# Eight-head attentions: two PSUM banks in turn for the value products, two instead of three for the turned tiles

## The chip, the cores and the metric

The kernel runs on one core of a Trainium2 chip. The metric is device time in microseconds (us). The engines of the core are TensorE (PE, with its weight loads as PEld), VectorE (DVE), ScalarE (ACT), GpSimd (POOL) and SyncE, which issues transfers. Matrix products leave TensorE into PSUM, which has eight banks of 128 partitions by 512 fp32 numbers; ScalarE and VectorE read them from there.

## The reference, cut to what matters

Two blocks of two layers each work on 1024 tokens of width 1024. Each of the four layers holds an attention with eight query heads of 64 columns, and the change touches these four alone.

```python
# first block, both layers: 8 query heads, 2 heads of keys and values, every key seen
sc = jnp.einsum('bgrqd,bgkd->bgrqk', qblk, kt)
p = jax.nn.softmax(sc, axis=-1)
return jnp.einsum('bgrqk,bgkd->bgrqd', p, vt)
...
# second block, both layers: 8 query heads, 1 head of keys and values, the keys of each row
# chosen (causal, top 256 by an index score)
sc = jnp.where(valid[:, :, None, :], sc, -jnp.inf)
p = jax.nn.softmax(sc, axis=-1).astype(v.dtype)
return jnp.einsum('bthk,btkd->bthd', p, v_sel)
```

The first block also has a differential attention of four heads in each layer. All is computed to fp32 precision, with each fp32 operand of a product split into a high and a low part.

## The kernel before, in words

`heads_phase` computes one attention of eight heads. It is called four times: with the tag `b_` in each layer of the first block, and with the tag `x_` in each layer of the second, where the mask is causal (`causal`). Each engine gets one instruction stream, written out by Python loops that run over the same step number `g` from -5 to 78 (`START` to `END`). The streams meet only in semaphores, so the order inside each stream is fixed.

A step `g` from 0 to 63 is one row tile: 128 queries of one head against all its keys (1024 in `b_`; 128 to 1024, growing with the query tile, in `x_`). Heads go in pairs: steps 16p to 16p+15 are the eight query tiles of the two heads of pair p, in turn. For one row tile:

- TensorE multiplies queries by keys into PSUM banks 0 to 3 (`scores`, line 1143), for two steps at once: the call for steps g+1 and g+2 stands in step g, for odd g.
- VectorE reads the scores, adds mask and minus maximum, and writes a row of probabilities to be (`shift`, line 1002). ScalarE takes the exponent (`exponent`, line 938), VectorE inverts the sum (`invert`, line 1010), GpSimd scales the row (line 1066).

Four row tiles of one head make a column block `n` of 512 queries. Its probabilities are turned (transposed) in tiles of 128 keys by 512 queries: four transposes of 128x128 into one bank (`turn`, line 1104). Each turned tile is then taken out of its bank twice: ScalarE copies the high part (`take`, line 922), and after it VectorE computes the low part from the bank and the high part (`take`, line 985). Two products multiply the tile's high and low part by the values (`product`, lines 1121 and 1122), summed over the block's tiles in one further bank. Once a block is summed, ScalarE reads that bank in two copies (`close`, lines 929 and 932), and GpSimd adds and gates it.

In `b_` every block has eight tiles, two in each step (below: the first and the second of the step). In `x_` the blocks of a head's first 512 queries have four tiles, one in a step, and those of its other 512 have eight, two in a step; so steps 8 to 15 of every 16 have one tile each, and steps 0 to 7 two, from step 8 on. At steps 8, 9, 24, 25, 40 and 41 one further tile is turned ahead of these, a "stack" of queries for the next pair (line 1098, taken out at lines 914 and 977). In `b_` steps 24 and 25 hold a stack of keys too, which makes it 24: keys, 25: keys and queries, 26: queries. `order` lists all turned tiles, stacks included, and `number` is a tile's place in it.

The streams run through a step in this order:

- TensorE: products of the tiles turned at step g-2; scores of g+1 if g is odd; turns of step g.
- ScalarE: takes of step g-1; `close` of a block, every fourth step (odd steps 13, 17, ...); exponent of g.
- VectorE: shift of g; inverse of g-1; takes of step g-1.

Banks: 0 to 3 hold scores, 4, 5 and 6 the turned tiles in rotation, 7 the products. Two waits guard them. The turn of tile i waits until VectorE has taken tile i-3, the last one in the same bank:

```python
elif i >= 3:
    before = order[i - 3]
    if before[0] == "stack":
        pe.wait_ge(stk_lo, moved[before])
    else:
        pe.wait_ge(tl_done, rank[before] + 1)
```

The first product of block n waits until both copies of block n-1 are done (`o_read`, 2n). Each `product` waits besides for the take of its own tile (`tl_done`).

The `b_` calls begin while the last steps of the differential attention (`diff_phase`, the `host`) still run on the same engines, and the first tiles wait on semaphores of that phase.

Of the kernel before, what the change touches and what calls it, by code (L numbers as in the profile page):

```python
# [17 lines left out]
ACT = mybir.ActivationFunctionType  # L18
# [16 lines left out]
HD = 64  # L35
# [718 lines left out]
def heads_phase(nc, env, tag, groups, queries, group_of, y_of, bias=None, load=(), ahead=(), gating=(), host=None):  # L754
# [7 lines left out]
    ps, ident = env["ps"], env["ident"]  # L762
    QB, RING, SLOTS, NS = 4, 16, 4, 4
# [50 lines left out]
    order = [e for g in range(START, END + 1) for e in plan[g]]  # L814
    number = {e: i for i, e in enumerate(order)}
# [6 lines left out]
    with ExitStack() as c:  # L822
# [4 lines left out]
        if host:  # L827
            nat, slots, biases, rows = host.at, host.at + 16 * S, host.at + 32 * S, host.at + 48 * S
# [9 lines left out]
            o_hi, o_lo = [at_host(name, [P, BANK], biases + o * S) for name, o in (("o_hi", 12), ("o_lo", 14))]  # L838
            ath, atl = host.ath, host.atl
            small = host.small  # L840
            zero, nm, sums, rr = small[:, 0:1], small[:, 8:8 + NS], small[:, 16:16 + NS], small[:, 24:24 + NS]
        else:
# [5 lines left out]
            o_hi, o_lo = sb("o_hi", [P, BANK]), sb("o_lo", [P, BANK])  # L848
            stg = [sb("stage", [P, T, 2 * HD]) for _ in range(NG)]
            zero = sb("zero", [P, 1])[:, :]  # L850
            ath = sb("attn_t_hi", [P, SLOTS, BANK], F32R)
            atl = sb("attn_t_lo", [P, SLOTS, BANK], F32R)
# [11 lines left out]
            return 1.0 if stacks[z][0][0] == "k" else HD ** -0.5  # L864

        def bank(e):
            return 4 + number[e] % (2 if host and number[e] < 4 else 3)

        def score_view(g):
            pair = 2 * (g % 2)  # L870
# [12 lines left out]
        with Phase(nc, joins=host.ph if host else None, continued=True) as ph:  # L883
# [18 lines left out]
            def _(act):  # L902
# [21 lines left out]
                def close(n):  # L924
                    rows = slice((n % 2) * HD, (n % 2 + 1) * HD)
                    act.wait_ge(pv_done, last_rank[n])
                    if n >= 1:
                        act.wait_ge(o_sum, n)
                    nc.scalar.activation(o_hi[rows, :], ps[0:HD, 7, :], ACT.Copy).then_inc(o_read, 1)  # L929
                    if n >= 1:  # L930
                        act.wait_ge(y_done, n)
                    nc.scalar.activation(o_lo[rows, :], ps[HD:2 * HD, 7, :], ACT.Copy).then_inc(o_read, 1)  # L932

                def exponent(g):
                    act.wait_ge(shifted, g + 1)
# [13 lines left out]
                before = steps[0](act)  # L949
                for _ in range(alone):  # L950
                    next(before)
                for g in range(START, END + 1):
# [6 lines left out]
                    n = (g - READ) // QB  # L959
# [115 lines left out]
            def _(pe):  # L1075
                def turn(e):
                    i = number[e]
                    if host and i < 4:
                        pe.wait_ge(host.tl_done, host.guest_rank + i + 1)
                    elif host and i == 5:  # L1080
                        pe.wait_ge(host.o_read, 2 * host.blocks)
                    elif host and i < 7:
                        pe.wait_ge(host.tl_done, host.products)
                    elif i >= 3:
                        before = order[i - 3]
                        if before[0] == "stack":
                            pe.wait_ge(stk_lo, moved[before])
                        else:
                            pe.wait_ge(tl_done, rank[before] + 1)
                    if e[0] == "stack":  # L1090
                        _, z, side = e
                        what, at = stacks[z][0]
                        if what == "k" and side == 0:
                            pe.wait_ge(staged, at + 1)
                        for i in range(QB):
                            t = QB * side + i
                            src = stg[at][:, t, :] if what == "k" else queries(at)[:, t, :]
                            mm = nc.tensor.transpose(ps[:, bank(e), i * P:(i + 1) * P], src, ident[:, :])
                    else:
                        _, n, j = e  # L1100
                        if j == 0:
                            pe.wait_ge(normed, rows_in(n)[-1] + 1)
                        for i in range(tile_lo(n, j) // P, QB):
                            mm = nc.tensor.transpose(ps[:, bank(e), i * P:(i + 1) * P],  # L1104
                                                     prob(rows_in(n)[i])[:, j * P:(j + 1) * P], ident[:, :])
                    mm.then_inc(turned, 1)

                def product(e):
                    if e[0] == "stack":
                        return  # L1110
                    _, n, j = e
                    kk, lo = rank[e], tile_lo(n, j)
                    pe.wait_ge(tl_done, kk + 1)
                    v = vv[group_at(n)][:, j, :]
                    if j == 0 and (n == 0 or group_at(n) != group_at(n - 1)):
                        pe.wait_ge(v_lo, group_at(n) + 1)
                    if j == 0 and n >= 1:
                        pe.wait_ge(o_read, 2 * n)
                    elif j == 0 and host:
                        pe.wait_ge(host.o_scaled, host.blocks)  # L1120
                    nc.tensor.matmul(ps[:, 7, lo:], v, ath[:, kk % SLOTS, lo:], start=(j == 0), stop=False)  # L1121
                    nc.tensor.matmul(ps[:, 7, lo:], v, atl[:, kk % SLOTS, lo:], start=False,  # L1122
                                     stop=(j == tiles(n) - 1)).then_inc(pv_done, 1)

                def scores(g):
# [21 lines left out]
                before = steps[3](pe)  # L1147
# [1609 lines left out]
```

## Time and profile before

| what | value |
|---|---|
| time, median of 3 runs | 3036.26 us (3034.1 to 3038.59) |
| time of the profiled execution | 3038.28 us |
| its span in the trace | 3036.4 us |
| TensorE granted clock, mean of the span | 0.945 of full speed |
| PE, DVE, ACT, POOL busy | 88%, 67%, 52%, 38% of the span |
| tiles turned for the probabilities, `b_` calls (1024 transposes) and `x_` calls (576 transposes) | line 1104 |

The profiled execution is one of its own; its time beside the span is what lies before the first and after the last instruction. Engine lines in the timelines give the start in the span, the length, the line of the kernel, the operation and its operands; in square brackets stands how long the engine was idle before it and what ended that. Rows that the profile merges carry a count (x8).

### The profile page before, as it was taken

The page shows a single profiled execution, that of the slowest core. Times are in us where ns is not written, and L with a number is a line of the kernel's source. Part 1 is how long each engine was busy: PE and PEld are TensorE (multiplying, and loading weights), DVE is VectorE, ACT ScalarE, POOL GpSimd, SP SyncE. Part 2 cuts the span into 40 slices and gives each one's busy share as a digit, 9 for nine tenths or more (in the row PEclk, how much of TensorE's full clock was granted, in tenths as well). Part 3 has the DMA queues.
Part 4 walks back from the last instruction along what each step waited for, and adds up shares of the span by engine and source line. Part 5 has one row for each costly group of instructions (what it writes and reads, how often), then busy time and mean ns, then how long its engine had stood idle before and what let it go on. Part 6 is the DMA issues. An engine that isn't in the chain of part 4 may idle for free. (4 is left out here: it accounts for less than half of the span.)

```text
span 3036.4 us, 41556 instructions
## 1 busy us (share of the span) xinstructions
PE 2676.1 (88%) x14032; PEld 2103.3 (69%) x14032; DVE 2028.4 (67%) x4312; ACT 1565.6 (52%) x3035; POOL 1161.2 (38%) x987
## 2 busy tenths in 40 slices
PE   6999888898999997989989897997889897997887
PEld 5877666676878775656777675775667685775666
DVE  4472487798434724867874358997767349997766
ACT  4221376698432114767872317684764317675751
POOL 0100276565101003765641002984731003984831
PEclk9999998999999998999999999998899899998998
DMA  4443210100324421001023101110032111110022
GB/s 126 120 146 102 87 41 8 42 1 29 132 70 136 138 78 57 21 8 42 1 68 127 53 18 32 42 46 25 1 125 77 59 25 25 46 42 25 1 90 83
DMA packets 90751, 181.94 MB, mean 60 GB/s; under 512 B 12552, under 2 KB 27912, under 8 KB 90504
## 3 DMA queue, kind: packets, MB, share of 16 engines
q1 hardware_dynamic: 74124, 150.69, 15.4%
q10 hardware_dynamic: 16416, 28.61, 3.1%
q8 instruction: 111, 1.82, 0.2%
q14 instruction: 100, 0.82, 0.1%
HBM read 149.87 MB, written 33.33 MB: 60 GB/s over the span
## 5 line engine op out<-in xcount | busy, mean ns | idle before, releaser
L1394 POOL TENSOR_SCALAR a_prob<-a_prob,a_ratio 128x1024 f32<-128x1024 f32 x64 | 72.1, 1127 | 511.1 <-DVE a_ratio L1353 511.1
L1849 PE MATMUL ps<-o_w_hi,hh 128*128 128x512 f32 x512 | 214.4, 419 | 24.3 <-DVE o_w_lo L1769 24.3
L2333 DVE TENSOR_SCALAR_CACHE_REDUCE select_rows<-masks,select_cuts 128x1024 bf16<-128x1024 int16 (+7 forms) x264 | 231.2, 879 | 0.2
L1849 PE MATMUL ps<-o_w_lo,hh 128*128 128x512 f32 x512 | 207.1, 404 | 0.0
L1849 PE MATMUL ps<-o_w_hi,hl 128*128 128x512 f32 x512 | 206.8, 404 | 0.0
L1825 POOL TENSOR_TENSOR o_rstd<-o_rstd,nhalf 128x1 f32<-128x1 f32 x56 | 46.7, 835 | 406.5 <-DVE o_rstd L1706 236.5
L1342 DVE CUSTOM_DVE_ANT_0 a_prob<-ps,a_bias 128x1024 f32<-128x1024 f32 x128 | 151.7, 1221 | 65.4 <-PE ps L1484 59.2
L750 PE MATMUL ps<-w_first,hh 128*128 128x512 f32 (+1 forms) x616 | 178.0, 375 | 19.4 <-DVE w_first L631 4.8
L1066 POOL TENSOR_SCALAR b_prob<-b_prob,a_guest_small 128x1024 f32<-128x1024 f32 x128 | 144.5, 1129 | 126.9 <-DVE a_guest_small L1010 124.3
L1002 DVE CUSTOM_DVE_ANT_1 b_prob<-ps,a_guest_small 128x1024 f32<-128x1024 f32 x128 | 155.9, 1218 | 31.1 <-PE ps L1143 31.1
L985 DVE TENSOR_TENSOR a_attn_t_lo<-ps,a_attn_t_hi 128x512 fp32r<-128x512 f32 x256 | 163.7, 680 | 14.2 <-ACT a_attn_t_hi L922 13.7
L2508 PE MATMUL ps<-hh,w_hi 128*128 128x512 f32 x384 | 154.4, 402 | 13.8 <-POOL w_lo L2471 6.8
L938 ACT ACTIVATE b_prob<-b_prob,a_guest_small 128x1024 f32<-128x1024 f32 x128 | 147.6, 1154 | 29.8 <-DVE a_guest_small L1002 29.5
L922 ACT ACTIVATE a_attn_t_hi<-ps 128x512 fp32r<-128x512 f32 x256 | 139.4, 599 | 35.7 <-PE ps L1104 34.8
L1297 ACT ACTIVATE a_prob<-a_prob,a_neg_max 128x1024 f32<-128x1024 f32 x128 | 146.1, 1148 | 17.9 <-DVE a_neg_max L1342 17.7
L1397 POOL TENSOR_TENSOR a_prob<-a_prob 128x1024 f32<-128x1024 f32 x64 | 152.6, 2384 | 5.3
L2508 PE MATMUL ps<-hh,w_lo 128*128 128x512 f32 x384 | 153.1, 399 | 0.0
L2508 PE MATMUL ps<-hl,w_hi 128*128 128x512 f32 x384 | 152.4, 397 | 0.0
L566 ACT ACTIVATE w_hi<-w_raw 128x512 fp32r<-128x512 f32 (+1 forms) x54 | 32.4, 600 | 228.9 <-PE ps L750 224.0
L750 PEld LDWEIGHTS ps<-w_first,hh 128*128 128x128 f32 x616 | 111.8, 191 | 44.8 <-issue 10.0
L1104 PE MATMUL ps<-ident,b_prob 128*128 128x128 f32 x1024 | 139.4, 278 | 3.0 <-DVE b_key_stack L977 1.9
L631 DVE TENSOR_TENSOR w_lo<-w_raw,w_hi 128x512 fp32r<-128x512 f32 (+1 forms) x54 | 35.2, 653 | 159.7 <-ACT w_hi L566 159.7
(380 smaller groups left out, 8145.1 us busy)
## 6 DMA issues: line engine op xcount, KB each, us to landing
w_early<-in_w_in SPq DMA_DIRECT2D x108, 256.0 KB, 2.8
ada_w<-in_w_ada ACTq DMA_DIRECT2D x96, 256.0 KB, 2.7
w_raw<-in_w_in SPq DMA_DIRECT2D x78, 256.0 KB, 2.8
ak<-gates SPq DMA_DIRECT2D x32, 256.0 KB, 3.7
xcur<-aq SPq DMA_DIRECT2D x16, 512.0 KB, 4.4
y<-xcur SPq DMA_DIRECT2D x16, 512.0 KB, 3.6
a_bias<-bias_tiles SPq DMA_DIRECT2D x8, 960.0 KB, 4.9
bq<-in_w_out SPq DMA_DIRECT2D x12, 512.0 KB, 4.2
```

What stands on the lines that cost most here:

```text
L750: mm = nc.tensor.matmul(o, lhs, rhs, start=(k == 0 and i == 0), stop=(k == K - 1 and i == 2))
L922: nc.scalar.activation(ath[:, kk % SLOTS, lo:], ps[:, bank(e), lo:], ACT.Copy).then_inc(th_done, 1)
L938: nc.scalar.activation(prob(g), prob(g), ACT.Exp, bias=nm[:, g % NS:g % NS + 1], scale=-1.0, accum_out=sums[:, g % NS:g % NS + 1]).then_in ...
L985: nc.vector.tensor_tensor(atl[:, kk % SLOTS, lo:], ps[:, bank(e), lo:], ath[:, kk % SLOTS, lo:].bitcast(F32), ALU.subtract).then_inc(tl_do ...
L1002: nc.vector.tensor_tensor_reduce(out=row_view(prob(g), g), in0=score_view(g), in1=added, scale=-1.0, scalar=3.0e38, op0=ALU.add, op1=ALU.m ...
L1066: nc.gpsimd.tensor_scalar(prob(b), prob(b), rr[:, b % NS:b % NS + 1], 0.5, ALU.mult, ALU.mult).then_inc(normed, 1)
L1297: nc.scalar.activation(row, row, ACT.Exp, bias=nm[:, g % NS, m:m + 1], scale=-1.0, accum_out=out).then_inc(exped, 1)
L1342: nc.vector.tensor_tensor_reduce(out=row, in0=scores_of(g, m), in1=bias, scale=-1.0, scalar=3.0e38, op0=ALU.add, op1=ALU.min, accum_out=nm ...
L1397: nc.gpsimd.tensor_tensor(row0(g), row0(g), row1(g), ALU.add).then_inc(combined, 1)
L1849: mm = nc.tensor.matmul(o, lhs, rhs, start=(k == 0 and i == 0), stop=(k == K - 1 and i == 2))
L2333: spare_free[z] = mark(nc.vector.tensor_scalar(spare[:, z, 0:(qb + 1) * P], values, against, None, op, ALU.add, accum_out=column(count_of, ...
L2508: mm = nc.tensor.matmul(ps[:, b, :], lhs, rhs, start=(k == 0 and i == 0), stop=(k == K - 1 and i == 2))
```

## The change

The products of block n go to bank 6 + n % 2, so two banks in turn, and the first product of block n waits for the copies of block n-2 instead of n-1. The turned tiles go to bank 4 + number % 2, so two banks instead of three, and a turn waits for the take of the tile two places before instead of three. The waits on the host phase are cut to fit: the `o_read` wait of tile 5 goes, and the products of blocks 0 and 1 both wait for `host.o_scaled`. No arithmetic changes.

```diff
         def bank(e):
-            return 4 + number[e] % (2 if host and number[e] < 4 else 3)
+            return 4 + number[e] % 2
...
-                    nc.scalar.activation(o_hi[rows, :], ps[0:HD, 7, :], ACT.Copy).then_inc(o_read, 1)
+                    nc.scalar.activation(o_hi[rows, :], ps[0:HD, 6 + n % 2, :], ACT.Copy).then_inc(o_read, 1)
...
-                    nc.scalar.activation(o_lo[rows, :], ps[HD:2 * HD, 7, :], ACT.Copy).then_inc(o_read, 1)
+                    nc.scalar.activation(o_lo[rows, :], ps[HD:2 * HD, 6 + n % 2, :], ACT.Copy).then_inc(o_read, 1)
...
                     if host and i < 4:
                         pe.wait_ge(host.tl_done, host.guest_rank + i + 1)
-                    elif host and i == 5:
-                        pe.wait_ge(host.o_read, 2 * host.blocks)
-                    elif host and i < 7:
+                    elif host and i < 6:
                         pe.wait_ge(host.tl_done, host.products)
-                    elif i >= 3:
-                        before = order[i - 3]
+                    elif i >= 2:
+                        before = order[i - 2]
...
-                    if j == 0 and n >= 1:
-                        pe.wait_ge(o_read, 2 * n)
+                    if j == 0 and n >= 2:
+                        pe.wait_ge(o_read, 2 * (n - 1))
                     elif j == 0 and host:
                         pe.wait_ge(host.o_scaled, host.blocks)
-                    nc.tensor.matmul(ps[:, 7, lo:], v, ath[:, kk % SLOTS, lo:], start=(j == 0), stop=False)
-                    nc.tensor.matmul(ps[:, 7, lo:], v, atl[:, kk % SLOTS, lo:], start=False,
+                    nc.tensor.matmul(ps[:, 6 + n % 2, lo:], v, ath[:, kk % SLOTS, lo:], start=(j == 0), stop=False)
+                    nc.tensor.matmul(ps[:, 6 + n % 2, lo:], v, atl[:, kk % SLOTS, lo:], start=False,
                                      stop=(j == tiles(n) - 1)).then_inc(pv_done, 1)
```

## Rows read from the trace of the kernel before

**Rows 1.** the page: span, then each engine’s busy time, share and instructions
```profile
span 3036.4 us, 41556 instructions
...
PE 2676.1 (88%) x14032; PEld 2103.3 (69%) x14032; DVE 2028.4 (67%) x4312; ACT 1565.6 (52%) x3035; POOL 1161.2 (38%) x987
```

**Rows 2.** what TensorE waited for before line 1121, whole span: us, times
```profile
  ACT b_o_lo L932: 2.1, 4
  ACT x_o_lo L932: 1.2, 4
```

**Rows 3.** three stretches: length, busy PE, PEld, DVE, ACT, POOL, granted clock, DMA
```profile
580.00:725.00 145.00, 140.48 (x936) 107.30 (x937) 130.01 (x262) 129.22 (x236) 88.05 (x75) 1.00 0.06 22
...
1399.00:1544.00 145.00, 140.50 (x936) 107.44 (x936) 129.99 (x262) 129.20 (x236) 88.05 (x75) 1.00 0.06 22
2762.00:2921.00 159.00, 126.78 (x808) 97.66 (x808) 107.78 (x299) 118.14 (x268) 105.91 (x110) 0.90 0.02 8
```

**Rows 4.** timeline of TensorE in a `b_` call: start, length, line, operation
```profile
604.72 1.66 PE L1143 MATMUL ps<-b_key_stack,b_query_stack 64*128 64x512 f32 x12 [0.15 <-DVE a_guest_small L1002]
606.31 1.09 PE L1104 MATMUL ps<-ident,b_prob 128*128 128x128 f32 x8
607.16 0.47 PE L1121 MATMUL ps<-a_attn_t_hi,b_values 128*128 128x512 f32 x1
...
608.17 1.04 PE L1104 MATMUL ps<-ident,b_prob 128*128 128x128 f32 x8
608.96 0.47 PE L1121 MATMUL ps<-a_attn_t_hi,b_values 128*128 128x512 f32 x1
...
610.12 1.66 PE L1143 MATMUL ps<-b_key_stack,b_query_stack 64*128 64x512 f32 x12
...
615.64 0.73 PE L1143 MATMUL ps<-b_key_stack,b_query_stack 64*128 64x512 f32 x4
```

**Rows 5.** timeline of VectorE in the same steps
```profile
607.64 1.28 DVE L985 TENSOR_TENSOR a_attn_t_lo<-ps,a_attn_t_hi 128x512 fp32r<-128x512 f32 x2
608.84 1.22 DVE L1002 CUSTOM_DVE_ANT_1 b_prob<-ps,a_guest_small 128x1024 f32<-128x1024 f32 x1
...
613.16 1.29 DVE L985 TENSOR_TENSOR a_attn_t_lo<-ps,a_attn_t_hi 128x512 fp32r<-128x512 f32 x2
```

**Rows 6.** timeline of ScalarE in the same steps
```profile
607.00 1.09 ACT L922 ACTIVATE a_attn_t_hi<-ps 128x512 fp32r<-128x512 f32 x2 [1.06 <-PE ps L1104]
...
610.16 0.59 ACT L929 ACTIVATE b_o_hi<-ps 64x512 f32<-64x512 f32 x1
```

**Rows 7.** timeline of TensorE, steps 24 to 26 of a `b_` call
```profile
621.42 1.66 PE L1143 MATMUL ps<-b_key_stack,b_query_stack 64*128 64x512 f32 x12
...
625.51 0.66 PE L1104 MATMUL ps<-ident,b_prob 128*128 128x128 f32 x4 [0.97 <-DVE b_key_stack L977]
...
629.25 0.96 PE L1143 MATMUL ps<-b_key_stack,b_query_stack 64*128 64x512 f32 x6
```

**Rows 8.** timeline of VectorE, step 25
```profile
620.98 0.67 DVE L977 SCALAR_TENSOR_TENSOR b_key_stack<-ps,b_key_stack 128x512 fp32r<-128x512 f32 x1
```

**Rows 9.** timeline of VectorE, then TensorE, end of a `b_` call
```profile
729.56 1.27 DVE L985 TENSOR_TENSOR a_attn_t_lo<-ps,a_attn_t_hi 128x512 fp32r<-128x512 f32 x2
...
730.28 0.65 PE L1104 MATMUL ps<-ident,b_prob 128*128 128x128 f32 x4 [0.33 <-DVE a_attn_t_lo L985]
```

**Rows 10.** timeline of VectorE and then TensorE in an `x_` call
```profile
2875.64 1.29 DVE L985 TENSOR_TENSOR x_attn_t_lo<-ps,x_attn_t_hi 128x512 fp32r<-128x512 f32 x2 [0.46 <-ACT x_attn_t_hi L922]
...
2817.05 0.63 PE L1104 MATMUL ps<-ident,x_prob 128*128 128x128 f32 x4 [2.42 <-POOL x_prob L1066]
...
2833.68 1.94 PE L1104 MATMUL ps<-ident,x_prob 128*128 128x128 f32 x8 [0.37 <-DVE x_attn_t_lo L985]
...
2854.01 0.63 PE L1104 MATMUL ps<-ident,x_prob 128*128 128x128 f32 x4 [1.20 <-POOL x_prob L1066]
...
2888.47 0.63 PE L1104 MATMUL ps<-ident,x_prob 128*128 128x128 f32 x4
```

## The prediction

> **What bounds the kernel now.** I read the page first, to see which engine is scarce: TensorE is busy 88% of the span, VectorE 67% [rows 1]. That average says little about the four calls that change, so I took the windows next. In the two `b_` calls TensorE is busy 140 of 145 us and VectorE 130, at full granted clock, and both calls show the same figures to 0.1 us [rows 3]; what is worked out for one holds for both. In the `x_` call both are looser and the clock is 0.90. Then the waits, for the one that the change removes: over the whole span TensorE stood idle 3.3 us, eight times, for the copies of the product bank [rows 2]. That is all the second product bank can give directly. What it costs to lose the third bank of turned tiles no row sums up, because that wait mostly does not exist yet, so the timelines decide.
>
> The timeline of a `b_` call shows a loop of two steps [rows 4 to 6]. I count from the start S of a `scores` call. In the loop that starts at 604.72 the turns of the odd step start at S+1.59, its four products at S+2.44, the turns of the even step at S+3.45 (608.17), their following four products at S+4.24 (608.96), and the next scores at S+5.40 (610.12). VectorE takes the two tiles of the odd step from S+2.92 to S+4.20 (607.64, x2, 1.28) and ends the odd step's shift at S+5.34 (608.84 + 1.22), which is what releases the next scores. The four products before them end at S+5.25 (608.96 + 1.01, the distance from 607.16 to 608.17). So TensorE has 0.15 us to spare in 5.40 us and VectorE sets the pace together with the scores. Every second loop also holds a `close` on ScalarE (610.16), which pushes the takes back to 613.16: that loop is 5.52 us (610.12 to 615.64).
>
> **The change part by part.**
>
> *Second product bank.* Removes the wait of the first product for the copies of the block before: at most 3.3 us [rows 2], nearly all at the ends of the calls, where ScalarE takes no tile while it copies, so that the next turn waits instead. I count it inside the tail below, as close to nothing. The copies themselves, 0.59 us each [rows 6], stay where they are. The host's waits only swap banks: the stream order already puts them behind it. Nothing is added to SP's or POOL's queues.
>
> *Two banks for turned tiles, plain loops.* A turn now waits for the take two places back. In a step of two tiles, the first turn waits for the take of the first tile of the step before, the second for the second. Before, the second waited only for the first tile's take, and the first for nothing new. For odd steps the next scores cover it, which run ahead of the turns: VectorE starts the even step's takes right behind the shift that releases these scores and is through with both 1.2 us after their start, and the turns come 1.59 us after it. For even steps nothing covers it. A turn starts 0.08 us after the take it waits for (729.56 and half of 1.27, against 730.28 [rows 9]), its product 0.40 us after it (half of 608.17 to 608.96). So the second turn starts at S+4.20+0.08 = S+4.28, the products at S+4.68, and after their 1.01 us the scores at S+5.69 in place of S+5.40: 0.29 us more. Behind the waiting turn on TensorE's queue stand the products and the scores, and for these VectorE waits; the start of its next shift moves with them, so nothing of it is won back.
>
> In the loop with a `close` the takes end at 613.16 + 1.29, S+4.33; ScalarE's close now starts 0.15 us later against S, because it starts when the last product is done, and the scores now follow the products without the old slack; exponent and takes come behind it on ScalarE: S+4.48. Turn S+4.56, products S+4.97, scores S+5.98, against 5.52: 0.46 us more. One call has 21 such loops with two turned tiles in each step (scores of steps 11 to 61, less the four intervals with stacks), 10 plain and 11 with a close: 10 x 0.29 + 11 x 0.46 = 8.0 us.
>
> *Steps with stacks.* With three tiles in a step, the third now needs the bank of the first tile of the same step, which VectorE takes only in the next step, behind a whole shift. The trace has this stall once per `b_` call already: step 25 has four tiles, its fourth needs the bank of its first, and TensorE stands 0.97 us for it [rows 7]. In step 24 the stack is taken at 620.98 + 0.61 [rows 8], that is S+5.95 from 615.64; the third turn starts at S+6.03, its products at S+6.43, the scores at S+7.44 instead of S+5.78 (621.42): 1.7 us more. The same in step 40: 1.7. In step 25 the third and fourth turn wait for the first and second (fourth turn S+4.65 instead of 4.09), and in step 26 the third waits behind the shift of 27 again: the fourth tile's take ends at S+6.6, the shift at S+7.8, the stack's take at S+8.4, the turn starts at S+8.5, its products at S+8.9, the scores at S+9.9 instead of S+7.83 (629.25): 2.1 more. Step 41 costs 1.0 (VectorE's shift sets the end there), steps 8 and 9 together 2.4; both are estimates, carried through the same timelines by the same prices. Sum 8.9 us per call.
>
> *Tail of a `b_` call.* After step 63 there is no shift; a bank goes round in the distances turn to copy (0.69, 606.31 to 607.00), copy to take (0.64, 607.00 to 607.64), take to turn (0.65 + 0.08). With the second turn 0.6 us behind the first, the two engines can no longer overlap as before, where a step took 0.79 us of turns and 1.01 of products; I get 2.0, and about 1.2 us at each close, against which stand the waits of the first product that go, 0.5 us each (2.1 in 4 [rows 2]). Carried through the nine steps: 2.2 us. One `b_` call: 8.0 + 8.9 + 2.2 = 19.1 us, both 38.
>
> *`x_` calls.* Where a step has one tile (steps 8 to 15 of 16), the take two places back is one that the products in front have waited for already: nothing. Steps 0 to 7 have two. There the first turn of step 2 waits for the take of the step before, whose pair runs 2875.64 to 2876.93 [rows 10]: the second turn starts at 2877.01 instead of 2876.37, 0.64 us; step 6 the same, step 4 0.15, the others nothing: 1.4 us in a pass. In the first two passes GpSimd's gating is later still, TensorE waits 2.42 and 1.20 us for it, which hides this. In the third (2888.47) the row names no wait, and the gap in front of it is about 0.2 us, so 1.2 us is lost [rows 10]; the last pass has no scores between and loses 1.8. Sum 3.0, both calls 6.
>
> **The sum** is 38 + 6 = 44 us on the profiled execution's 3038.3 us (span 3036.4, 1.9 around it). That execution lies 2.0 us above the median of the runs; on the median, 3036.3 + 44 = 3080.3 us. No price here is of an operation that the trace lacks; the unknown is how much of the waits is hidden. Lowest: plain loops lose nothing, because the ends of matmuls are modelled and the true slack may be larger than 0.15 us, leaving 2 x (8.9 + 2.2) + 6 = 28 us. Highest: each of 25 loops loses a full spacing of two takes, 0.64 us, on top of everything else: 2 x (16 + 8.9 + 2.2) + 6 = 60 us.
>
> The clock in the `b_` calls is at full speed throughout [rows 3], and in an `x_` call, after a stretch with waits, eight transposes took 1.94 us [rows 10] against 1.04 in [rows 4], the lower of the two levels (1.2 GHz against 2.4). The Trainium skill (TensorE: Matmul & The Clock Gate, "A second HAM failure mode: psum-queue depth-cycling") says that a kernel which cycles PSUM banks each iteration idles TensorE in short gaps often enough that its clock swings between its levels. By that rule the `b_` calls would come out far slower than by the sum above; with three banks cycling they show none of it, so the trace does not bear it out so far.
>
> **The rivals.**
>
> *The waits hide (not slower).* If the second turn's lateness were taken up, by TensorE running ahead or VectorE's takes coming earlier than its own shift, the change would give its 3.3 us and no more: 3033 to 3036 us. For it: VectorE and scores set the pace, not the turns. Against: the slack is 0.15 us, and the second turn is 0.43 us late. It decides only if that lateness stays under 0.15 us.
>
> *Only the stack steps cost.* 28 us, 3064. For it: the stall is in the trace already. Against: the plain loops' arithmetic.
>
> *The clock falls.* If the new gaps, about 0.4 us in each loop and up to 1.7 us at stacks, brought the lower level to one loop in eight of the `b_` calls (7 of 52), each such loop pays about double for 16 transposes (1.8 us), 8 products (1.5) and the scores (1.5), 4.8 us: 33 us on top, 3113. Against: gaps like these stand at step 25 in both calls, and the windows there give 1.00.
>
> **How the numbers follow.** As reckoned 0.72; only the stacks 0.13; hidden 0.08; clock 0.07. I predict 3080 us. The range takes the two middle cases whole and their bounds, 3056 to 3102, and leaves out the hidden case and the clock, 0.15 together, with a little for errors. A change of under 0.2% (6 us) can't be told from none. Faster by more would need twice what the waits hold: 0.02. Same 0.06, slower 0.92.
>
> **What would show it.** In the timeline of a `b_` call scores 5.7 and 6.0 us apart in turn, with TensorE idle before the second turn of even steps, ended by VectorE's take; at steps 24 and 40 a stall of 1.7 us before the last turn; line 1121 no longer waiting for ScalarE's copies; each `b_` call about 19 us longer, each `x_` about 3; busy times unchanged. The prediction is wrong if the scores stay 5.40 apart, if the granted clock in the `b_` windows leaves 1.00, or if the turns of odd steps wait too.

## The result, and the profile after the change

The changed kernel takes 3086.4 us (median of 4 runs, 3084.4 to 3090.2), the kernel before 3035.2 us in the same comparison (4 runs, 3028.1 to 3038.6). The ratio is 1.0171, 95% interval 1.0150 to 1.0191: slower by 1.7%, some 46 to 58 us. The profiled execution took 3086.5 us, span 3084.2 us, 47.8 us more than before.

The page after, span and busy times, against [rows 1]:

```profile
span 3084.2 us, 41554 instructions
...
PE 2700.9 (88%) x14032; PEld 2091.0 (68%) x14032; DVE 2031.0 (66%) x4312; ACT 1572.8 (51%) x3035; POOL 1159.1 (38%) x987
```

The work is the same: 14032 matmul records, and VectorE, ScalarE and GpSimd within 8 us of before. TensorE's busy time rose by 25 us all the same, in the `b_` calls by 10.5 us each at an unchanged clock: matmuls overlap in the record, and less so around a wait (the eight even turns below count 1.25 us instead of 1.04). A page like this can't say why the kernel is slower. What TensorE waited for before the turns of the attention tiles can. The view is taken on the matmul side alone, because a wait on the weight-load side (PEld) lies in part beside running matmuls (us, times); first before the change, line 1104, then after, line 1102:

```profile
  POOL x_prob L1066: 6.8, 4
  DVE x_attn_t_lo L985: 4.7, 10
  DVE b_key_stack L977: 1.9, 2
  DVE a_attn_t_lo L985: 0.7, 2
  DVE b_query_stack L977: 0.2, 1
```

```profile
  DVE x_attn_t_lo L985: 13.2, 23
  DVE b_query_stack L977: 13.0, 10
  DVE a_attn_t_lo L985: 9.1, 28
  DVE x_query_stack L977: 5.9, 6
  DVE b_key_stack L977: 4.9, 4
  POOL x_prob L1066: 1.7, 3
```

The waits for VectorE's takes (lines 985 and 977) went from 7.5 us to 46.1, in 71 places instead of 15. The wait for GpSimd shrank from 6.8 to 1.7. Before the products (line 1119) the waits for ScalarE's copies [rows 2] are gone, all 3.3 us, and the wait for takes fell from 21.4 us to 12.4:

```profile
  DVE x_attn_t_lo L985: 12.4, 16
```

These sums name the new wait, and don't add up to the loss: part of it stands on the weight-load side (the second tile's turns in a `b_` loop), part is only moved from the products to the turns. The timelines below do add up.

Two loops of two steps in a `b_` call, against [rows 4]. TensorE, the scores first, then odd turns, even turns, even products:

```profile
643.67 1.67 PE L1141 MATMUL ps<-b_key_stack,b_query_stack 64*128 64x512 f32 x12
645.28 1.09 PE L1102 MATMUL ps<-ident,b_prob 128*128 128x128 f32 x8
...
647.53 1.25 PE L1102 MATMUL ps<-ident,b_prob 128*128 128x128 f32 x8 [0.23 <-DVE a_attn_t_lo L985]
648.54 0.47 PE L1119 MATMUL ps<-a_attn_t_hi,b_values 128*128 128x512 f32 x1
...
649.64 1.65 PE L1141 MATMUL ps<-b_key_stack,b_query_stack 64*128 64x512 f32 x12
...
653.29 1.25 PE L1102 MATMUL ps<-ident,b_prob 128*128 128x128 f32 x8
654.30 0.48 PE L1119 MATMUL ps<-a_attn_t_hi,b_values 128*128 128x512 f32 x1
...
655.41 0.98 PE L1141 MATMUL ps<-b_key_stack,b_query_stack 64*128 64x512 f32 x6
```

and VectorE in the second of them:

```profile
651.34 1.23 DVE L1002 CUSTOM_DVE_ANT_1 b_prob<-ps,a_guest_small 128x1024 f32<-128x1024 f32 x1 [0.87 <-PE ps L1141]
...
652.57 1.27 DVE L985 TENSOR_TENSOR a_attn_t_lo<-ps,a_attn_t_hi 128x512 fp32r<-128x512 f32 x2
```

Eight turns, two tiles, take 1.25 us now where they took 1.04 (608.17 in [rows 4]). Both tiles wait for a take, which the weight loads of the even turns in the second loop show:

```profile
653.29 0.42 PEld L1102 LDWEIGHTS ps<-ident,b_prob 128*128 128x128 f32 x4 [0.48 <-DVE a_attn_t_lo L985]
...
653.89 0.42 PEld L1102 LDWEIGHTS ps<-ident,b_prob 128*128 128x128 f32 x4 [0.18 <-DVE a_attn_t_lo L985]
```

The loops are 5.97 us with a close (643.67 to 649.64) and 5.77 without (649.64 to 655.41). VectorE now stands idle 0.87 us for the scores in each loop, where it stood 0.50 to 0.58 us in the same two loops before. The same two stretches as [rows 3] (the second begins 17 us earlier in its call than before, since the call itself starts later):

```profile
580.00:725.00 145.00, 134.41 (x848) 95.29 (x848) 117.42 (x235) 119.09 (x213) 79.47 (x68) 1.00 0.06 23
1399.00:1544.00 145.00, 130.26 (x813) 91.75 (x814) 113.75 (x230) 113.49 (x203) 78.72 (x71) 0.99 0.07 23
```

Every engine does less in these 145 us, at a clock as high as before. The 0.99 isn't the change's doing. Around the scores of step 7 the granted clock is 0.50 for some 3.5 us in every `b_` call, before the change too (570 to 573 and 1389 to 1392), and only the shifted window takes that in. With the window at the same place of the call, it is before that has the 0.99 (first row before, second row after):

```profile
1382.00:1527.00 145.00, 138.73 (x912) 105.64 (x914) 126.97 (x259) 126.11 (x229) 89.85 (x80) 0.99 0.07 23
```

```profile
1416.00:1561.00 145.00, 134.01 (x844) 94.86 (x846) 117.81 (x235) 119.31 (x214) 79.75 (x68) 1.00 0.07 23
```

No engine became the bound: they wait for each other in turn.

Steps 24 to 26, against [rows 7], TensorE:

```profile
626.43 0.66 PE L1102 MATMUL ps<-ident,b_prob 128*128 128x128 f32 x4 [1.15 <-DVE b_key_stack L977]
...
627.94 1.65 PE L1141 MATMUL ps<-b_key_stack,b_query_stack 64*128 64x512 f32 x12
...
631.92 1.25 PE L1102 MATMUL ps<-ident,b_prob 128*128 128x128 f32 x8 [1.30 <-DVE b_key_stack L977]
...
636.40 0.66 PE L1102 MATMUL ps<-ident,b_prob 128*128 128x128 f32 x4 [1.15 <-DVE b_query_stack L977]
...
637.91 1.66 PE L1141 MATMUL ps<-b_key_stack,b_query_stack 64*128 64x512 f32 x12
```

One stall of 0.97 us became three of 1.15 to 1.30 us, one in each step with a stack, and what lies around them shifts too.

Because each call's timeline starts alike, the loss can be read off by place. Starts of `scores` in the first `b_` call, us; the last column is what was lost since the row above:

| scores of step | before | after | lost up to here | since the row above |
|---|---|---|---|---|
| first | 534.71 | 534.71 | 0 | |
| 7 | 569.01 | 569.00 | 0 | 0 |
| 11 | 581.06 | 583.77 | 2.71 | 2.7, stacks of steps 8 and 9 |
| 23 | 615.64 | 620.38 | 4.74 | 2.0, six loops |
| 25 | 621.42 | 627.94 | 6.52 | 1.8, stack of 24 |
| 27 | 629.25 | 637.91 | 8.66 | 2.1, stacks of 25 and 26 |
| 39 | 662.31 | 673.25 | 10.94 | 2.3, six loops |
| 41 | 668.11 | 680.82 | 12.71 | 1.8, stack of 40 |
| 43 | 674.51 | 688.37 | 13.86 | 1.2, stack of 41 |
| 61 | 724.10 | 741.34 | 17.24 | 3.4, nine loops |
| last product starts | 748.8 | 768.5 | 19.7 | 2.5, tail |

The second `b_` call repeats it (1.8 and 2.1 us at steps 24 to 26, 19.8 us in all). The `x_` calls lost 4.1 and 5.9 us. That is 49.6 us; the rest of the kernel differs by -1.8 us.

From here on, the length of a call is that from the start of its first scores to the start of its last product. The recorded expectations partly count from the first probabilities to the last product, which gives 1 to 3 us less.

| kernel | `b_` calls, us | `x_` calls, us | median, us | ratio to before, 95% |
|---|---|---|---|---|
| before | 214.1, 214.2 | 153.4, 151.3 | 3032.4 to 3037.1 | 1 |
| changed | 233.8, 233.9 | 157.5, 157.2 | 3086.4 | 1.0150 to 1.0191 |
| changed, once more | 234.0, 234.0 | 158.7, 154.7 | 3085.4 | 1.0151 to 1.0179 |
| one product bank | 234.0, 234.0 | 158.7, 156.6 | 3084.4 | 1.0151 to 1.0181 |
| `b_` calls alone | 234.0, 235.5 | 153.2, 151.4 | 3073.5 | 1.0120 to 1.0150 |
| `x_` calls alone | 214.1, 214.2 | 157.5, 157.2 | 3047.1 | 1.0031 to 1.0061 |
| stacks in bank 6 | 227.6, 226.2 | 155.4, 157.0 | 3067.4 | 1.0093 to 1.0127 |
| query stack later | 213.5, 213.6 | 153.5, 151.3 | 3035.6 | 0.9990 to 1.0008 |
| one turn bank | 379.5, 389.7 | 230.3, 240.8 | 3556.1 | one run |
| `x_` stall filled | 234.0, 235.4 | 154.9, 154.0 | 3083.4 | 1.0143 to 1.0174 |
| `x_` start filled | 214.0, 214.0 | 153.3, 152.8 | 3040.4 | 1.0002 to 1.0019 |

The kernel before had a median of 3032.4 us beside the first four experiments and of 3036.7 to 3037.1 beside the others, so ratios and call lengths say more than differences of medians.

### The profile page after: what moved, and what is told of

Same layout as the page of the kernel before. It is cut to its first block and busy times, and to the rows that moved or that the text cites. A ratio compares the mean times of both kernels' runs of the same rounds, so it can differ in the third digit from the quotient of the medians.

```text
span 3084.2 us, 41554 instructions
## 1 busy us (share of the span) xinstructions
PE 2700.9 (88%) x14032; PEld 2091.0 (68%) x14032; DVE 2031.0 (66%) x4312; ACT 1572.8 (51%) x3035; POOL 1159.1 (38%) x987
## 5 line engine op out<-in xcount | busy, mean ns | idle before, releaser
L1102 PE MATMUL ps<-ident,b_prob 128*128 128x128 f32 x1024 | 154.0, 284 | 28.2 <-DVE b_query_stack L977 13.0
L1102 PEld LDWEIGHTS ps<-ident,b_prob 128*128 128x128 f32 x1024 | 109.5, 141 | 88.6 <-DVE a_attn_t_lo L985 49.0
L2506 PE MATMUL ps<-hh,w_hi 128*128 128x512 f32 x384 | 153.2, 399 | 13.7 <-POOL w_lo L2469 6.7
L2506 PE MATMUL ps<-hh,w_lo 128*128 128x512 f32 x384 | 153.3, 399 | 0.0
L2506 PE MATMUL ps<-hl,w_hi 128*128 128x512 f32 x384 | 153.2, 399 | 0.0
```

Source lines behind the costliest of these rows:

```text
L2506: mm = nc.tensor.matmul(ps[:, b, :], lhs, rhs, start=(k == 0 and i == 0), stop=(k == K - 1 and i == 2))
```

## The experiments

**One product bank.** The third turn bank goes, the second product bank doesn't come; bank 6 is unused.

```diff
-            return 4 + number[e] % (2 if host and number[e] < 4 else 3)
+            return 4 + number[e] % 2
...
-                    elif host and i == 5:
-                        pe.wait_ge(host.o_read, 2 * host.blocks)
-                    elif host and i < 7:
+                    elif host and i < 6:
                         pe.wait_ge(host.tl_done, host.products)
-                    elif i >= 3:
-                        before = order[i - 3]
+                    elif i >= 2:
+                        before = order[i - 2]
```

> Turned tiles in two banks as in the change, products in bank 7 alone with the old wait. Theory (all the loss is the third turn bank): about 50 us slower than the kernel before, that is as slow as the changed kernel or up to 3 us slower still, since the removed wait held 3.3 us in all. Rival (the second product bank gives back a good part of the loss): clearly slower than the changed kernel, 60 us or more above before.

Measured: 3084.4 us, a ratio of 1.0166 where the changed kernel has 1.0171 and 1.0165, and `b_` calls equal to 0.2 us. The whole loss is that of the third turn bank, and the second product bank gives nothing that the times or the traces can show. Nor is there much left for it to give: of the 3.3 us of waits for copies [rows 2] this kernel, with two turn banks and one product bank, has only 1.0 us, in four places.

**The change in the `b_` calls alone, and in the `x_` calls alone.**

```diff
+        two = host is not None      # the other kernel: host is None
+        turns_ahead = 2 if two else 3
+        def sum_bank(n):
+            return 6 + n % 2 if two else 7
...
-                    elif i >= 3:
-                        before = order[i - 3]
+                    elif i >= turns_ahead:
+                        before = order[i - turns_ahead]
```

> The whole change in the two b_ calls alone. Theory: 38 us slower than before, 19 in each call. Rival (the loss sits in the x_ calls, where the clock is lower): under 20 us.

> The whole change in the two x_ calls alone. Theory: 6 us slower than before by the prediction's sum, 9 by the first look at the trace of the changed kernel; together with the run of the b_ calls alone it makes the whole. Rival (the calls act on each other, through the clock or through late transfers): the two do not add up to the whole, by more than 5 us.

Measured: +19.9 and +21.3 us in the `b_` calls (41 us, against a ratio that says 36 to 45), and +4.1 and +5.9 in the `x_` calls (10 us; 9 to 18 by the ratio), each with the other pair at its old length to 0.3 us. By the lengths of the calls the parts add up: the `b_` calls as forecast, the `x_` calls above it.

The 21.3 is 1.5 us more than in the other traces, and all of it lies in one place, the scores of step 9 (a loop for `b_` calls alone, second call):

```profile
1414.40 0.66 PE L1110 MATMUL ps<-ident,b_prob 128*128 128x128 f32 x4 [1.91 <-DVE b_query_stack L983]
...
1415.85 2.92 PE L1149 MATMUL ps<-b_key_stack,b_query_stack 64*128 64x512 f32 x12
```

The granted clock from 1416 to 1419 is 0.50. The first trace of the changed kernel has the same stall (1.92 us, 1411.47), and its scores behind it take 1.66 us (1412.92). Of the ten `b_` calls traced with two turn banks and no bank for stacks, two fell like this, this one and the second in the kernel with the `x_` stall filled (235.4 us). So in the `b_` calls the clock can fall behind a new wait too, and then costs 1.5 us.

**Stacks in bank 6.** Two banks in turn for the attention tiles, and for stacks (after the first) a bank of their own.

```diff
         def bank(e):
-            return 4 + number[e] % (2 if host and number[e] < 4 else 3)
+            if e[0] == "attn":
+                return 4 + rank[e] % 2
+            return 4 + number[e] % 2 if number[e] < 4 else 6
```

> Turned tiles of probabilities in banks 4 and 5 in turn, stacks (but the first four) in bank 6, products in bank 7 with the old wait. Theory (plain loops 8 us and stack steps 9 us in each b_ call): the loops and the tail stay slow, the third tile of a step no longer waits for the first, so about 30 us above before instead of 50. Rival 1 (stack steps cost no more than others): still about 48. Rival 2 (only stack steps cost): under 12.

The waits follow the banks. Measured: by the ratio the whole is 28 to 39 us above before, near the 30 expected, and the `b_` calls are at +13.5 and +12.0 us, between the extremes. The attention tiles' loops keep their price, since they still take two banks in turn: the loop of 612.03 to 617.99 is 5.96 us. What is saved is most of the stack steps, 6 to 8 us per call of the 9.6. Not all: the two stack sides of one step now share one bank, and the second waits for the take of the first (TensorE, step 25):

```profile
627.87 0.97 PE L1103 MATMUL ps<-ident,bq 128*128 128x128 f32 x4 [1.83 <-DVE b_key_stack L979]
628.64 1.91 PE L1109 MATMUL ps<-ident,b_prob 128*128 128x128 f32 x8
```

The eight turns behind this wait took 1.91 us, at a granted clock of 0.51 (628 to 631), where the second call ran them at the upper level: that is the 1.4 us between the two calls.

So both extremes fall by one run, that only the stacks cost and that they cost nothing: with most of their price gone, 25.6 of 39.6 us remain in the `b_` calls.

**The query stack one step later**, with three turn banks: no step turns four tiles any more.

```diff
-            lead += 1
+            lead += 1 if p == 0 else 2
         stacks.append((("q", p), lead))
```

> The kernel before, with the stack of the third head pair's queries turned one step later (steps 26 and 27 instead of 25 and 26), so that no step turns more than three tiles. My theory says that even three turn banks run out in the one step that turns four tiles (an attention tile, the side of a stack, and two more), where the trace of before shows TensorE idle for 0.97 us behind VectorE's take of b_key_stack, once in each of the b_ calls. Expected: that wait is gone from both b_ calls, each of these calls is 0.5 to 1.5 us shorter (first of the probabilities to last product), and the whole is 1 to 2 us shorter than the kernel before, which its times can hardly tell from no change. Rival: the later stack is late for the scores that read it, or its take falls into VectorE's fuller step, and the calls are no shorter or up to 2 us longer.

Measured: the wait for `b_key_stack` is gone, and scores of step 27 follow those of 25 by 6.77 us (620.36 to 627.13) instead of 7.83 [rows 7]. But a `b_` call is only 0.6 us shorter, as the moved tile takes its time in the next loop, and the whole is not to be told from before (ratio 0.9999). This run beats the changed kernel, and isn't faster than the kernel before.

**One turn bank**: a second dose.

```diff
-            return 4 + number[e] % (2 if host and number[e] < 4 else 3)
+            return 4 + number[e] % 2 if host and number[e] < 4 else 4
...
-                    elif i >= 3:
-                        before = order[i - 3]
+                    elif i >= 1:
+                        before = order[i - 1]
```

> The kernel before with a single turn bank for all but the first tiles (products in one bank, as before): a second dose of the suspected cause. Theory: each turn now waits for VectorE's take of the tile just before it, so what the third bank cost in some steps is paid at every tile: three to four turns in a loop of two steps, of which each waits about 0.9 to 1.3 us (the time from a turn's end to the end of its take), less the products and scores that now lie in between. I expect 2 to 4 us more per loop of two steps in the b_ calls, 25 or so of these in each of two calls, 100 to 200 us in all, and some tens of us in the x_ calls: 3180 to 3300 us. Rival, that the loss of the change came from VectorE's or TensorE's load and not from the turn's wait: less than 3100 us.

Measured: 3556 us, 256 us above the top of what I expected. TensorE in step 24 and after it:

```profile
660.40 0.66 PE L1102 MATMUL ps<-ident,b_prob 128*128 128x128 f32 x4 [1.41 <-DVE a_attn_t_lo L985]
...
668.79 2.51 PE L1141 MATMUL ps<-b_key_stack,b_query_stack 64*128 64x512 f32 x12
```

The price of a wait is near what I had taken, 1.41 us. On the matmul side the turns of the first `b_` call waited 117 us for takes, in 95 places, 1.24 us each; with 128 attention tiles in a call the sum was to be made by tiles, and I had made it by loops, 2 to 4 us for each. Most of the rest is the clock, which I had left out: over the two `b_` calls the granted clock was 0.87 and 0.84, before 0.98, and TensorE's busy time grew by 52 and 62 us for the same matmuls (in the changed kernel, at the clock of before, by 10.5). The calls grew by 165 and 176 us, so the waits account for some two thirds of it. The direction is clear and the effect is far from linear: the third bank is worth some 50 us, the second 470 more.

**The changed kernel once more**, as a check on differences of a few microseconds.

> The changed kernel itself, beside the others of this job: 3080 to 3090 us, and phases of 231 us (b_ calls) and 156 us (x_ calls), as in its first profile. Any other number would mean that the differences of a few us that I read between jobs are not to be trusted.

Measured: 3085.4 us. The `b_` calls repeat to 0.2 us; the `x_` calls don't: 158.7 and 154.7 us, where the first trace has 157.5 and 157.2. So a single `x_` call tells nothing below some 2.5 us, and the forecast of 3.0 for each has to be judged on both traces. Where the second of them lost its 3.5 us: TensorE, the turn at the end of the first, second and third pass, against 2.42 us, 1.20 us and no wait in [rows 10]:

```profile
2859.74 0.63 PE L1102 MATMUL ps<-ident,x_prob 128*128 128x128 f32 x4 [0.76 <-POOL x_prob L1066]
...
2896.66 0.63 PE L1102 MATMUL ps<-ident,x_prob 128*128 128x128 f32 x4 [0.46 <-POOL x_prob L1066]
...
2933.05 0.66 PE L1102 MATMUL ps<-ident,x_prob 128*128 128x128 f32 x4
```

From the first of these rows to the second it is 36.92 us (36.96 before, 2817.05 to 2854.01): nothing is lost, GpSimd's gating hides it, and the wait for it shrinks. From the second to the third it is 36.39 against 34.46: 1.9 us lost, where I had 1.2. What is left for the last pass is 1.5, where I had 1.8. The third pass ran at a granted clock of 0.91 there, 0.95 before; the first trace of the changed kernel has both passes at the 0.95 of before and loses some 1.7 us in each (36.11 against 34.46, 32.92 against 31.19).

**The stall in the `x_` calls filled.** The kernel with one product bank, and six turns of the unit matrix into the unused bank ahead of the turn that waits for the second side of a stack.

```diff
                         if before[0] == "stack":
+                            if host is None and before[2] == 1:
+                                for _ in range(6):
+                                    nc.tensor.transpose(ps[:, 6, 0:P], ident[:, :], ident[:, :])
                             pe.wait_ge(stk_lo, moved[before])
```

> The kernel with two turn banks and one products bank, and in the x_ calls alone six extra turns of the unit matrix into the unused bank 6, ahead of the turn that waits for the second side of a stack. They add TensorE work of about 0.9 us into a wait of 0.6 to 1.2 us, three times in each x_ call; no value is changed. The x_ calls lost 4.1 and 5.9 us to the change, where I had forecast 3.0 each. Theory: part of the rest is TensorE's clock. In the trace of the changed kernel the granted clock is 0.50 to 0.65 in the scores that follow this wait (2.26, 2.41 and 2.61 us for twelve matmuls that took 1.31 to 1.49 us before). If the idle time of that wait is what brings the clock down, filling it keeps the twelve at about 1.5 us, and the x_ calls come out 1 to 3 us shorter than with the same banks unfilled (157.7 and 155.5 us), although TensorE does more. Rival: the clock falls by something else (the low stretches lie in other places too, in the kernel before as well), and the fillers change nothing or cost up to 1 us each: x_ calls of 156 to 160 us.

The scores behind that wait, in the first trace of the changed kernel:

```profile
2866.72 2.41 PE L1141 MATMUL ps<-x_key_stack,x_query_stack 64*128 64x448 f32 x12 [0.25 <-DVE x_neg_max L1002]
...
2904.50 2.61 PE L1141 MATMUL ps<-x_key_stack,x_query_stack 64*128 64x448 f32 x12 [0.25 <-DVE x_neg_max L1002]
```

and with fillers:

```profile
2858.71 0.82 PE L1087 MATMUL ps<-ident 128*128 128x128 f32 x6
...
2861.36 1.49 PE L1144 MATMUL ps<-x_key_stack,x_query_stack 64*128 64x448 f32 x12 [0.26 <-DVE x_neg_max L1002]
...
2897.48 1.48 PE L1144 MATMUL ps<-x_key_stack,x_query_stack 64*128 64x448 f32 x12 [0.25 <-DVE x_neg_max L1002]
```

The whole of the second `x_` call by windows (first probabilities to last product), before, changed, changed once more, filled; the last three columns are granted clock, DMA share, GB/s:

```profile
2769.40:2919.70 150.30, 121.87 (x786) 93.69 (x786) 105.01 (x295) 113.68 (x261) 105.91 (x110) 0.91 0.00 1
```

```profile
2811.20:2967.40 156.20, 128.95 (x786) 95.35 (x786) 105.72 (x295) 114.58 (x261) 105.60 (x110) 0.89 0.00 1
```

```profile
2812.10:2965.80 153.70, 124.97 (x786) 91.97 (x786) 105.45 (x295) 114.69 (x261) 105.81 (x110) 0.92 0.00 1
```

```profile
2807.20:2960.50 153.30, 126.07 (x810) 92.94 (x810) 105.54 (x295) 114.63 (x261) 105.92 (x110) 0.93 0.00 1
```

Measured: with TensorE given more to do, the `x_` calls came out at 154.9 and 154.0 us, 4.2 us over the kernel before in sum, against 8.7 to 10.5 in the four traces with the same turn banks and no fillers. The fillers stand in five places of a call, not three: the condition also holds ahead of the first scores and ahead of the first tile of probabilities, where the changed kernel waits for no stack.

The three waits themselves lie ahead of the scores of steps 11, 27 and 43. At step 11 (a wait of 0.5 to 0.6 us) the scores ran at the upper level in every trace. At steps 27 and 43 (1.2 us) they took 2.13 to 2.61 us in 12 places of 16 in the four traces without fillers, and 1.48 or 1.49 us in all four places with fillers. But in the second call of the changed kernel's second trace both ran at the upper level too (1.49 us each), with nothing filled, while its first call had both low. The 2.26 us that the expectation counts belongs to step 9, ahead of the first wait, where the low stretch of the lead-in lasts longer.

So the fillers go with fewer falls, and that this wait is what brings them isn't shown. Before the change TensorE stood idle 1.41 us at the same places, ahead of the products (2822.35 and 2859.32) instead of the turn, and only one of the four scores behind it was slow. The fillers' gain is read from one trace, and by the whole time (3083.4 against 3085.4 us, intervals overlapping) it is not established.

**The start of the `x_` calls filled**, in the kernel before: 24 turns of the unit matrix ahead of the first stack, 4 ahead of each of the scores of steps 2 to 8.

```diff
+                        if host is None and number[e] == 0:
+                            for _ in range(24):
+                                nc.tensor.transpose(ps[:, 4, 0:P], ident[:, :], ident[:, :])
...
+                        if host is None and g <= 8:
+                            for _ in range(4):
+                                nc.tensor.transpose(ps[:, 6, 0:P], ident[:, :], ident[:, :])
                         pe.wait_ge(shifted, g)
```

> The kernel before, with its banks as they were, and extra turns of the unit matrix in the lead-in of the x_ calls alone, where no tile is turned and TensorE idles between the scores (0.61, 1.68, 1.20 and 1.46 us, at a granted clock of 0.50 for the first 13 us): 24 of them ahead of the first stack, in an idle time of 7.75 us, and 4 ahead of each of the scores of steps 2, 4, 6 and 8. No value is changed. Theory: it is the idle time ahead of TensorE that brings the clock down in the x_ calls, as the filled wait of the experiment before this one showed, so the fillers bring it up and the stacks' turns (1.97 and 1.91 us) and the scores (1.01 to 1.97 us) shrink towards half; x_ calls 2 to 5 us shorter each than 152.3 and 150.3 us with what lies ahead of them, 4 to 9 us in all, 3027 to 3033 us where the kernel before runs 3035. Rival: the scores there lie behind VectorE and ScalarE, or the clock stays down with TensorE at less than half busy, and the time is that of the kernel before within 2 us, or longer by the fillers' time.

```profile
2777.17 0.62 PE L1149 MATMUL ps<-x_key_stack,x_query_stack 64*128 64x256 f32 x6
2777.73 0.66 PE L1136 MATMUL ps<-ident 128*128 128x128 f32 x4
2779.87 0.80 PE L1149 MATMUL ps<-x_key_stack,x_query_stack 64*128 64x384 f32 x6 [1.49 <-DVE x_neg_max L1002]
...
2781.86 1.65 PE L1149 MATMUL ps<-x_key_stack,x_query_stack 64*128 64x512 f32 x6 [0.61 <-DVE x_neg_max L1002]
```

Measured: a ratio of 1.0002 to 1.0019, if anything slower. The first scores did run at the upper level (0.62 us for six, 1.01 unfilled), but the next ones were still released by VectorE, and at the fourth scores the clock was down again (1.65 us), fillers or not. The rival holds: in the lead-in neither the clock nor TensorE sets the time, and I take no gain from it. The theory also took the filled wait of the experiment before as proof of what brings the clock down, which it was not.

## Why the prediction was right, step by step

The forecast was 3080 us, slower, range 3056 to 3102. The case "as reckoned" happened. Term by term, per call (measured: the table of places, and call lengths):

| term | forecast, us | measured, us |
|---|---|---|
| 21 loops of a `b_` call | 8.0 | 7.7 |
| stack steps 24; 25 and 26; 40; 41 | 1.7; 2.1; 1.7; 1.0 | 1.8; 2.1; 1.8; 1.2 |
| stack steps 8 and 9 | 2.4 | 2.7 |
| tail of a `b_` call | 2.2 | 2.5 |
| one `b_` call | 19.1 | 19.7 and 19.8 |
| one `x_` call | 3.0 | 4.1 and 5.9; 5.3 and 3.5 |
| both pairs | 44 | 49.6 and 48.5 |

*Second product bank*: right, worth nothing. The waits of [rows 2] went, and the kernel without that bank runs as fast; most of them go with the two turn banks alone.

*Plain and close loops*: the mechanism is right, the takes end at S+4.20 as said (652.57 + 1.27, from 649.64). Two prices were off, and offset each other. Even products to scores is 1.11 us (654.30 to 655.41), not 1.01, so a plain loop costs 0.37 instead of 0.29. And a close loop was 5.52 to 5.54 us before in three places only, 5.62 to 5.72 in the others (634.65 to 640.27 is one), so it costs 0.33 to 0.44, 0.39 in the mean, instead of 0.46. The count was off by one as well: 11 loops are plain and 10 have a close, not 10 and 11. One loop of the 21 lost only 0.06: it was 7.16 us long already (586.46 to 593.62), with other waits in it. That the sum is right to 0.3 us is in part luck.

*Stack steps*: right to 0.1 us where they were followed through the timeline, 0.2 and 0.3 low where they were estimated (41; 8 and 9). The third turn of step 24 starts 6.05 us behind the scores (626.43, from 620.38), where 6.03 was forecast. The sign given for it, a stall of 1.7 us, was worded wrongly: 1.7 is what the loop loses, the stall itself is 1.15.

*`x_` calls*: this is the term that was mis-sized, 6 us forecast, 10.0 and 8.7 measured. The places were right. In the second call of the first trace the two passes that ran at the clock of before (0.95) lost some 1.7 us each, forecast 1.2 and 1.8. The other 2.5 us lie in the first two passes, 1.7 and 0.8 us, where the forecast had nothing; the granted clock was 0.81 and 0.86 there, before 0.86 and 0.91. The second trace has these two passes at 0.87 and 0.95 and loses nothing in them. So the third pass was taken 0.5 us too short, and the rest goes with the clock. What makes the clock lower in one trace than in the next is open. I had counted the clock as a rival for the `b_` calls alone, and gave it no term in the `x_` calls, where rows of before already showed it falling after waits.

*The clock in the `b_` calls*: it isn't "at full speed throughout", as the prediction says. The rows behind that begin at 580, and around 571 the clock is down, before and after the change. So the sign that the clock in the windows leaves 1.00 came up in form, at 0.99, and means nothing (see the windows at the same place of the call). Nor did the busy times stay as forecast: TensorE's grew by 25 us.

*Rivals*. "The waits hide" fell: 0.37 us in nearly every loop. "Only the stack steps cost" fell by the run with the stacks in bank 6. "The clock falls" fell for the `b_` calls as a cost of 33 us: in the changed kernel the clock is as before there, and two of ten calls with these banks have one more low stretch, worth 1.5 us.

## What to carry to other kernels

Count the tiles that a step turns against the banks that they rotate through, in the order of the queues: a bank fewer than the largest step needs costs a whole step's shift each time, but even two banks for steps of two tiles lose time, because the second turn waits for a take that ends late in the step. A wait that a profile shows for one resource (3.3 us for product copies) says how much a bank can give there, and the bank's worth where it is must be worked out from the timeline, since the wait that it prevents isn't in the trace. And multiply a price by the number of tiles, not of loops, and ask what the added waits may do to the clock: with one turn bank a good part of what the `b_` calls lost is matmuls at the lower level.

## What the runs showed of the hardware

Many short waits left TensorE's clock up in the `b_` calls: with two banks and a wait in each loop, the granted clock is 1.00 and 0.99, as before. With one bank, and TensorE idle 1.41 us ahead of one tile after the other, the same call shows 0.87:

```profile
560.00:925.00 365.00, 235.71 (x1186) 158.09 (x1185) 177.82 (x329) 177.97 (x300) 117.12 (x105) 0.87 0.04 15
```

and twelve matmuls of the scores take 2.51 us in places, instead of 1.66. The Trainium skill (TensorE: Matmul & The Clock Gate, "A second HAM failure mode: psum-queue depth-cycling") describes a clock that swings between its levels in a kernel that cycles through PSUM banks, because TensorE idles briefly between groups of matmuls. The loops here that cycle through three or two banks show no such swing from 580 to 725; the kernel that turns all its tiles in one bank does.

Between these the clock is not the same from one call to the next. Behind the same stall of 1.9 us it fell in two of ten `b_` calls, and behind those of 1.2 us in the `x_` calls it was at the lower level in 12 places of 16. I had not expected that the same program, profiled twice, would spend a different share of an `x_` call at the lower level, and that this moves the call by 2.5 us (157.2 against 154.7), while a `b_` call without such a fall repeats to 0.2 us. What decides it no run here shows.
